# Idle products on TensorE in the first block's attention: 512 columns round the first scores, 128 columns in front of each later unit with sinks

## The reference

```
o_a = sliding_window_sink_attn(...)   # 8 heads of 64, window 128, a sink in the softmax
o_b = indexer_sparse_attn(...)        # 4 heads of 64, the 128 best keys by an index score
o_c = mla_attn(...)                   # 4 heads of 64 + 32, causal
mix = concatenate([o_a, o_b, o_c]);  x = layer_norm(ALPHA * x + mix @ w_out[l], ...)
```

## Time and profile before

| | |
|---|---|
| median of 3 runs | 3644.04 us (3640.45 to 3646.99) |
| the profiled execution | 3640.77 us, its span 3639.0 us |
| PE busy | 3385.7 us (93%) |
| DVE busy | 1957.4 us (54%) |
| ACT busy | 1400.2 us (38%) |
| mean granted PE clock | 0.941 |

### The profile page before, as it was taken

How to read it: one execution, slowest core, us unless ns; L and a number is a source line. 1 busy time by engine, 2 the same in 40 slices (tenths; PEclk the granted TensorE clock), 3 DMA queues, 4 the chain that set the end, 5 groups by cost and what they waited for, 6 DMA issues and landing times.

```text
span 3639.0 us, 41894 instructions
## 1 busy us (share of the span) xinstructions
PE 3385.7 (93%) x14724; PEld 2639.8 (73%) x14724; DVE 1957.4 (54%) x3052; ACT 1400.2 (38%) x2056; POOL 384.3 (11%) x233
## 2 busy tenths in 40 slices
PE   7799898997998898999997999999999989889998
PEld 5567677775676777788875788877887767668886
DVE  4753687557536876554546543456354443455353
ACT  3443567534434666322222322233223444432221
POOL 2101032322010222200010100010001000010000
PEclk9869999998598999999999999999999999899999
DMA  3101399611011998132322232324233212013232
GB/s 114 50 1 59 105 318 317 217 50 55 1 59 58 307 318 271 50 98 91 100 64 66 74 103 88 99 70 143 92 97 117 87 35 70 24 50 101 92 95 78
DMA packets 174980, 389.59 MB, mean 107 GB/s; under 512 B 11312, under 2 KB 70064, under 8 KB 174192
## 3 DMA queue, kind: packets, MB, share of 16 engines
q1 hardware_dynamic: 173424, 377.45, 32.3%
q0 software_dynamic: 1408, 10.23, 0.8%
HBM read 381.34 MB, written 6.29 MB: 107 GB/s over the span
## 4 chain that ended last, share of the span: by engine, by line
PE 71%; DVE 12%; DMA 8%; ACT 5%; DVEq 2%; issue 2%; POOL 0%; POOLq 0%; ACTq 0%; SPq 0%
PE ps L545 18%; PE ps L547 18%; PE ps L546 18%; DMA gate_up_stage<-in_w_gu 8%; PE ps L659 4%; DVE moe_lo L1809 4%; PE ps L681 3%; PE ps L665 2%; ACT moe_hi L1048 2%; PE ps L761 2%; PE ps L636 1%; PE ps L724 1%; PE ps L627 1%; ACT w_hi L1048 1%; PE ps L829 1%
## 5 line engine op out<-in xcount | busy, mean ns | idle before, releaser
L1466 DVE TENSOR_TENSOR w_lo<-w_stage,w_hi 128x1024 fp32r<-128x1024 f32 (+3 forms) x310 | 398.3, 1287 | 833.9 <-ACT w_hi L1048 832.8
L545 PE MATMUL ps<-xs_hi,w_hi 128*128 128x512 f32 (+2 forms) x1952 | 778.9, 399 | 53.2 <-DVE w_lo L1466 17.7
L1048 ACT ACTIVATE w_hi<-w_stage 128x1024 fp32r<-128x1024 f32 (+3 forms) x350 | 382.0, 1093 | 1032.3 <-PE ps L547 1020.9
L547 PE MATMUL ps<-xs_hi,w_lo 128*128 128x512 f32 (+2 forms) x1952 | 771.2, 395 | 0.0
L546 PE MATMUL ps<-xs_lo,w_hi 128*128 128x512 f32 (+2 forms) x1952 | 771.0, 395 | 0.0
L545 PEld LDWEIGHTS ps<-xs_hi,w_hi 128*128 128x128 f32 (+2 forms) x1952 | 369.1, 189 | 155.1 <-issue 39.1
L547 PEld LDWEIGHTS ps<-xs_hi,w_lo 128*128 128x128 f32 (+2 forms) x1952 | 368.8, 189 | 85.8
L546 PEld LDWEIGHTS ps<-xs_lo,w_hi 128*128 128x128 f32 (+2 forms) x1952 | 370.0, 190 | 82.9
L1809 DVE TENSOR_TENSOR moe_lo<-gate_up_stage,moe_hi 128x1024 fp32r<-128x1024 f32 x224 | 270.1, 1246 | 125.0 <-ACT moe_hi L1048 124.6
L1048 ACT ACTIVATE moe_hi<-gate_up_stage 128x1024 fp32r<-128x1024 f32 x224 | 226.6, 1053 | 147.6 <-DMA gate_up_stage<-in_w_gu 141.2
L547 PE MATMUL ps<-h_hi,w_lo 128*128 128x512 f32 x704 | 278.1, 395 | 0.0
(11 more groups left out here) (346 smaller groups left out, 5105.5 us busy)
## 6 DMA issues: line engine op xcount, KB each, us to landing
gate_up_stage<-in_w_gu SPq DMA_DIRECT2D x112, 1024.0 KB, 5.8
w_stage<-in_f_gu SPq DMA_DIRECT2D x174, 512.0 KB, 3.6
down_stage<-in_w_dn SPq DMA_DIRECT2D x112, 512.0 KB, 6.1
w_stage<-in_f_dn SPq DMA_DIRECT2D x64, 704.0 KB, 4.0
w_stage<-in_w_in SPq DMA_DIRECT2D x30, 512.0 KB, 3.6
w_stage<-in_d_qk SPq DMA_DIRECT2D x24, 512.0 KB, 3.5
w_stage<-in_w_out SPq DMA_DIRECT2D x16, 512.0 KB, 3.5
w_stage<-in_d_v SPq DMA_DIRECT2D x12, 512.0 KB, 3.6
```

The lines of the kernel that those rows point to most:

```text
L545: pe.matmul(o, lh, rh, start=start, stop=False)
L547: return pe.matmul(o, ll, rh, start=False, stop=stop)
L1048: copy = lambda o, i: nc.scalar.activation(o, i, ACT.Copy)
L1466: tt(w_lo[:, s, 0:n], stage[:, s, 0:n], w_hi[:, s, 0:n].bitcast(F32), ALU.subtract).then_inc(w_split, 1)
```

## The change

`keep_clock` gets a third argument, the width in blocks of 128 columns. In `attend(l)`, two idle products of 512 columns stand before the scores of the first three units and four behind them, all into bank 4. In front of the transposes of each later A unit (n = 1 to 31) stands one idle product of 128 columns, into the bank (4 or 5) that the transposes will overwrite. Nothing else changes; the other engines' orders stay as they are.

```diff
-            def keep_clock(n, b=7):
+            def keep_clock(n, b=7, w=NT):
                 for _ in range(n):
-                    pe.matmul(ps[:, b, :], ident[:, :], ident[:, :].unsqueeze(1).to_broadcast([P, NT, P]), start=True, stop=True)
+                    pe.matmul(ps[:, b, 0:w * P], ident[:, :], ident[:, :].unsqueeze(1).to_broadcast([P, w, P]), start=True, stop=True)
...
+                keep_clock(2, 4)
                 for n in range(3):
                     scores(UN[n], n, S_BANKS)
+                keep_clock(4, 4)
                 for n in range(N + 5):
                     if n < N:
+                        if n > 0 and BA[UN[n]["B"]]["sinks"]:
+                            keep_clock(1, 4 + n % 2, 1)
                         pe.wait_ge(p_exp, c0 + n + 1)
                         transposes(UN[n], n, prob, 4 + n % 2, S_RING)
```

## The result

The changed kernel takes 3591.65 us, median of 4 runs (3590.9 to 3597.59), beside 3642.82 us for the kernel before (4 runs, 3640.45 to 3646.99). The ratio is 0.987, 95% interval 0.9852 to 0.9889. That is 51 us faster; 3602 was predicted, 3582 to 3634 as the range. The profiled execution took 3591.55 us, 49.2 us less than that of before; the gain foreseen for it was 38.9.

A forecast was written before the change was run, and what follows sets the result against it. PE's own work at half clock was taken as the bound. Per layer 59.6 us plus 2.55 at the start replaced 81.3 and 82.0, saving 38.9 us in all: 3640.8 to 3602, range 3582 to 3634.

The forecast's parts named there:

- The clock and the mechanism: First block's attention: gaps at its start lose the full clock; filling them with 5.1 us of products keeps it.
- Until 168 us it was granted in full: First layer's attention start: the clock was full until 168 us, then 0.50 until the C units.
- nothing before the C units brings it back: First block's attention: a clock lost in batch 0 or at a batch end stays lost until the C units.
- The two products ahead at a cost of 0: Two 512-column products before the first scores cost 0, hidden by DVE's weight split; without that cover 1.7 us a layer.
- The four behind: Four 512-column products behind the first scores take 3.4 us, making the first transpose 2.55 us late in each layer.
- The units: A units at full clock with their idle product: 1.66 us for 256 keys, 1.11 for 128 keys.
- The wait for DVE at batch ends: PE waits 1 us for DVE in each of batches 1 to 3, 3.0 us a layer; masks 3.15 us apart.
- the turns of rows: Three turns of finished rows in batches 1 to 3, about 0.5 us each, 1.5 us a layer.
- Never holds: Rival: the clock falls again in batch 0, small products cost 13.6 us a layer, time 3673; chance 0.12.
- Part of the way: Rival: the clock falls, likely at a batch end; from batch 2 on in one layer 22 us, 3624; chance 0.14.
- DVE becomes the bound: Rival: DVE's masks and rounds set the pace at 2.0 us a unit, 16 us lost, 3618; chance 0.08.
- The skill's rule: Clock granted by TensorE's recent busyness; read with profile busy time it opposed the change, but the prediction trusted the rows.

## Why the prediction was right, and by how much it was off

- **The clock and the mechanism** were read rightly. A stage whose PE was "busy" for 30.00 of 30.00 us stood at half clock, and products that compute nothing made it faster. That both kinds are needed is now shown: without the small ones the clock lasts 4 and 6 us, without the large ones it is gone at the first transpose. Two things about it are not shown: why A units can't win the clock back, and whether a small product helps by what it computes or by the time that it puts between the others (at full clock a unit of 128 keys takes 0.9 us without it and 1.17 with it).
- **"Until 168 us it was granted in full"** holds only for the ten microseconds that the prediction looked at. From 150 to 157 us the kernel before stood at 0.50 as well. There the clock came back: from 153.27 us PE computed products of 512 columns back to back (L545 to L547), and behind 157.7 us they run at full clock. So PE's own work can win the clock back; it is the work of the A units that did not in 78 us. In every profile that lost the clock it came back only once the scores are those of the C units, three units ahead of the C units themselves. Where no small products run there (before, large ones only, units 1 to 3 only) that was at units 35 to 38, in six layers; where they do (small ones only, two ahead only) it was at units 30 to 32, in three layers, one of them at 964.5 us. That speaks for the small products helping there too, and the prediction's "nothing before the C units brings it back" is off by up to two units in these two kernels.
- **The two products ahead at a cost of 0** was wrong as a term. The weight split hides them from DVE, whose first mask does not wait for them, but not from PE: the four products behind the scores start that much later, and the first transpose with them. The run without the two shows 4.15 us to the first transpose instead of 6.06, so they cost 1.9 us a layer, and they were not needed.
- **The four behind.** The first transpose comes 170.44 - 164.38 = 6.06 us after the stage's start, against 3.25 before: 2.8 us a layer where I had 2.55. That sum was nearly right, since I had let the four begin at 167.1, but it belongs to all six: 0.9 us is left for the four by themselves.
- **The units.** Predicted 1.66 and 1.11 us, measured 1.71 and 1.17. The idle product costs 0.28 and not 0.22: between other products it does not run as tightly as the sixteen in a row from which I priced it. Units with the C units' narrow scores took 1.11, and the last of them, with no idle product after it, 0.84, not 1.44. I had priced that score product of 128 columns at 0.40 by the rows of the B units; it takes 217.45 - 217.23 = 0.22:

```profile
217.23 0.39 PE L659 MATMUL ps<-k_c,q_c 96*128 96x128 f32 x2
217.45 0.56 PE L681 MATMUL ps<-v_a,prob_t 128*128 128x64 f32 x4
```

- **The wait for DVE at batch ends** is the step that failed: I charged 3.0 us for three batch ends and 0.5 for the rounds. Batches 1 to 3 took 39.9 us where that part of the sum had 43.7, and batch 0 9.73 for 10.0. Of the 3.8 us the wait is 3.0: no wait of PE shows there at all. The narrow scores are 1.3 and the turns of rows 0.3 (2.10 - 1.71 = 0.39 us each, not 0.5), and the units themselves took 0.8 more than priced. DVE's masks there still lie 3.14 us apart after the change:

```profile
196.91 0.48 DVE L1579 CUSTOM_DVE_ANT_0 prob<-ps,mask_a,neg_sinks 128x256 f32<-128x256 f32 x1 [0.91 <-issue]
...
200.05 0.47 DVE L1579 CUSTOM_DVE_ANT_0 prob<-ps,mask_a,neg_sinks 128x256 f32<-128x256 f32 x1
```

  The distance was right; what PE has in hand was not. The loop computes scores three units ahead, and at 1.71 us a unit the two units I counted would already have been 3.4 us. A wait of 1 us on top came from no row. The run without rounds agrees, 39.90 us either way. The waits exist where units are short: ahead of the values PE idles 0.79 and 1.01 us among the first C units. Those four units took 5.93 us where I had 5.9, by luck: the waits were 1.8 us where I had 1, and the units themselves shorter.
- **Together**: 55.56 for 59.6 us, 4.0 a layer or 8.1. Another 0.8 comes from C units which the second layer had run at half clock, the start takes back 0.5, and 1.9 lie outside the attentions, with no cause shown: that is the 10.3 us by which the gain was larger than the sum.
- **The rivals.** "Never holds" was priced at 3673; the run with the small products alone gave 3667. Without the 5.1 us for the start, which that run doesn't have, the price is 3668. That it comes so near is in part luck: a small product took 0.53 us at half clock and not 0.44, which alone makes 5.6 us more, and the run was timed beside a kernel before of 3638.7 and not 3640.8. "Part of the way" was priced at 3624 for a loss from batch 2 on in one layer; with only the two ahead it gave 3623. That they agree is luck: there the layer lost its clock from the third unit on, and the start was cheaper. What held is the price of a unit at half clock, 3.15 - 1.71 = 1.4 us. Both courses were real, a few products away from the change. "DVE becomes the bound" is refuted for the A units with their small products; without these, waits of PE appear.
- **The skill's rule.** Read with the profile's busy time, the rule of the Trainium skill (TensorE: Matmul & The Clock Gate, "What's actually happening") spoke against the change. The runs contradict that reading: fully busy PE stood at either clock. Another place of the Trainium skill (Perfetto Trace Analysis, "Identifying the Most-Contended Engine") says that matmul busy time is not a good measure of how close a kernel is to the roofline, because matmuls are pipelined. It does not speak of the clock; the rows here, which read 30.00 of 30.00 at both clocks, show that busy time does not tell the granted clock either.

Not settled: why the same code behind the second attention takes from 2593.7 to 2603.8 us, and with it several us of the differences between whole times above; and what in the A units' work keeps it from winning the clock back.

## What to carry to other kernels

Look at the granted clock by stage before believing a busy PE, and compare small differences between kernels stage by stage too: a stage of small products can read 100% busy and stand at half clock for 80 us, because it once lost its clock in a gap of 2.6 us at its start. Filling that gap costs nothing where PE waits anyway; then find by experiment which units can't hold the clock by themselves, and feed only those. Time such a kernel in many runs, since near the edge the same program falls to one side or the other.

## What the runs showed of the hardware

- The same instructions behind gaps of 0.92 and 0.91 us kept the clock in one layer and lost it in the other, and from run to run the time moved between 3618 and 3687 us. One profile shows one such outcome out of several.
- Holding a clock takes less than winning it back: with small products in batch 0 only, the A units of 256 keys kept 1.00 to their end, and with none, after the clock had fallen in batch 0, the same units stood at 0.50 for as long as they ran. That is shown for this mixture of products, and not why it is so.
- At full clock a score product of 128 columns took 0.22 us on 96 partitions (217.23 to 217.45 us, changed kernel) and 0.41 on 64 (172.27 to 172.68, the run without the two ahead); one of 256 columns 0.43 and 0.63 (221.97 to 222.40 and 183.68 to 184.31, changed kernel). Fewer partitions were not cheaper here. Why is not shown.
